# A 16-expert block: the loop over pairs of experts written out, and the last rows finished and waited for in another way

## Chip, core and metric

The kernel runs on one core of one Trainium2 chip. A core has five engines with an instruction stream each: TensorE (PE), VectorE (DVE), ScalarE (ACT), GpSimd (POOL) and SyncE (SP). The metric is the time in microseconds from the start of the program to its end on that core; the median of several runs counts.

## What is computed

One encoder layer over two sequences of 512 and 1024 tokens, width 1024: a mixer of attention and a state-space scan, a layer norm, then a feed-forward part in which each of 16 experts chooses its tokens, and a second layer norm. Only the feed-forward part and what follows it are touched:

```
aff = softmax((h @ w_router), axis=-1)
gate_vals, tok_idx = lax.top_k(aff.T, cap)              # per expert: 64 and 128 tokens of the two sequences
xg = h[tok_idx]
hid = silu(einsum('ecd,edf->ecf', xg, w_gate)) * einsum('ecd,edf->ecf', xg, w_up)
out = einsum('ecf,efd->ecd', hid, w_down) * gate_vals[..., None]
y = zeros_like(h).at[tok_idx.reshape(-1)].add(out.reshape(-1, d))
x = layer_norm(ALPHA * x + y, ln2_g, ln2_b)
```

`d` is 1024 and each expert's inner width is 2816, that is 22 chunks (`FCH`) of 128.

## The kernel before

`stage_experts` (from L1806) does the feed-forward part. Operands are float32 split into a high part and a remainder (`whi`, `wlo`; `xgT`, `hid` hold both), so that one product is made of several matmuls.

**An expert.** On TensorE it has 22 gate-and-up chunks (`gate_up`, L2043 and L2044, into `gu`) and 22 down chunks (`down`, L2055 to L2059, into `dns` and `dnp`). After chunks 0 and 1 it transposes the next expert's gathered tokens (`fill_tokens`, L2031 and L2032); these write into the banks of `dns`, so they wait (`row_done`) until the expert before has had its results read out. That read-out is `rows`: four ScalarE multiplications (L2172, L2175) and two VectorE operations (L2277) which stand at the start of the next expert, ahead of its first chunk. ScalarE copies each weight tile to `whi` (L2142), VectorE makes `wlo` (L2248), and SyncE loads 1056 weight tiles of 512 KB in a loop of its own. GpSimd gathers tokens and scatters results with indirect transfers.

**Loops.** The helper `experts` is used by TensorE, ScalarE and VectorE. Expert 0 and expert 15 are written out; experts 1 to 14 are a hardware loop (`Fori`, L1906) of seven turns with two experts in its body, so each of the three engines jumps back six times, at the ends of experts 2, 4, 6, 8, 10 and 12. Inside each expert the chunks 4 to 21 are a second hardware loop (L1915), three turns of six chunks.

**The end.** While expert 15 runs, GpSimd loads the accumulated rows tile by tile and ScalarE and VectorE normalise all 12 tiles as if expert 15 had chosen nothing. The rows that expert 15 did choose (`base_s`, 128 rows, and `base_p`, 64 rows) are done again at the very end by `last_rows`: VectorE adds expert 15's results (L2300; L2301 and L2304), ScalarE makes the mean (L2180) and the sum of squares (L2184), GpSimd the root in two steps (L1990, L1992), VectorE applies `gain` (L2282) and `shift` (L2287), and GpSimd writes the rows over the stored ones with two indirect transfers (L2022), after the stores of the 12 tiles have landed. GpSimd then waits for these two (`fix_out`). The stage closes (L1806) with a drain of each engine and a barrier over all five.

Of the kernel before, what the change touches and what calls it, by code (L numbers as in the profile page):

```python
# [1784 lines left out]
def stage_experts(nc, dram, res):  # L1785
# [20 lines left out]
    with ExitStack() as ctx:  # L1806
# [31 lines left out]
        rstd = m.sb("rstd", [P, NT + 2])  # L1838

# [60 lines left out]
        fix_out = m.sem("fix_out")  # L1900
        block = ctx.enter_context(nc.Block())
# [35 lines left out]
        def _(pool):  # L1937
# [48 lines left out]
            def root(n, ps=P):  # L1986
                of = (slice(0, ps), slice(n, n + 1))
# [4 lines left out]
                pool.tensor_tensor(rstd[of], rstd[of], half[0:ps], ALU.pow).then_inc(rstd_ready, 1)  # L1992
# [30 lines left out]
            pool.wait_ge(fix_out, 32)  # L2023
# [113 lines left out]
        def _(act):  # L2137
# [39 lines left out]
            def mean(n, of, ps=P):  # L2177
                if n >= 2:
                    act.wait_ge(var_ready, n - 1)
                act.activation(junk[n % 2][0:ps], of, ACT.Identity, scale=-1.0 / D, accum_out=nmean[0:ps, n:n + 1]).then_inc(mean_ready, 1)  # L2180

            def variance(n, of, ps=P):
                act.wait_ge(mean_ready, n + 1)
                act.activation(junk[n % 2][0:ps], of, ACT.Square, bias=nmean[0:ps, n:n + 1], accum_out=var[0:ps, n:n + 1]).then_inc(var_ready, 1)  # L2184
# [9 lines left out]
            def last_rows():  # L2194
# [17 lines left out]
        def _(dve):  # L2212
# [67 lines left out]
            def gain(n, of, ps=P):  # L2280
                dve.wait_ge(var_ready, n + 1)
                dve.scalar_tensor_tensor(of, of, nmean[0:ps, n:n + 1], ln[0:ps, 0, :], ALU.add, ALU.mult).then_inc(gained, 1)  # L2282

            def shift(n, of, ps=P):
                dve.wait_ge(gained, n + 1)
                dve.wait_ge(rstd_ready, n + 1)
                dve.scalar_tensor_tensor(of, of, rstd[0:ps, n:n + 1], ln[0:ps, 1, :], ALU.mult, ALU.add).then_inc(o_ready, 1)  # L2287
# [9 lines left out]
            def last_rows():  # L2297
                dve.wait_ge(gran_mm, GR * EXPERTS)
                dve.wait_ge(base_in, 32)
                dve.scalar_tensor_tensor(base[0][:], flat(dns), res["gates"][0][:, LAST:], base[0][:], ALU.mult, ALU.add).then_inc(y_ready, 1)  # L2300
# [3 lines left out]
                dve.tensor_tensor(base[1][:], base[1][:], plo[:], ALU.add).then_inc(y_ready, 1)  # L2304
                for i in range(2):
                    gain(NT + i, base[i][:], rows_of[i])
                    shift(NT + i, base[i][:], rows_of[i])
# [180 lines left out]
```

## Time and profile before

| | us |
|---|---|
| runs: 3512.11, 3512.74, 3518.86; median | 3512.74 |
| the profiled execution's own time | 3510.34 |
| its span, first to last instruction | 3508.2 |
| TensorE busy | 3376.6 (96%) |
| VectorE busy | 2343.7 (67%) |
| ScalarE busy | 1902.0 (54%) |
| GpSimd busy | 433.9 (12%) |
| mean granted TensorE clock | 0.983 of full speed |

The span is 2.1 us shorter than the time of the same execution, so a change of the span is read as the same change of the time. Expert 0's first matmul starts at 1019 us, expert 15's last at 3485.6 us: the feed-forward part is 70% of the span.

### The profile page before, as it was taken

To read this page: it belongs to the slowest core of one execution; us is meant where nothing else is said; L and a number is where in the kernel's file an instruction comes from. 1 tells how busy PE (TensorE), PEld (TensorE's weight loads), DVE (VectorE), ACT (ScalarE), POOL (GpSimd) and SP (SyncE) were. 2 spreads that over 40 slices of the span, in tenths; PEclk is the share of its full clock that TensorE was granted. 3 is DMA by queue.
4 is the path that set the end of the run, shared out by engine and by line. 5 is a ranking of instruction groups with operands and counts; after the bars stand their busy time and mean duration, and the time that the engine had idled before them with its cause. 6 is when DMAs were issued, how large, how long until landed. Compare 5 with 4: busy or idle time off the path is not lost.

```text
span 3508.2 us, 61800 instructions
## 1 busy us (share of the span) xinstructions
PE 3376.6 (96%) x20362; PEld 3094.5 (88%) x20362; DVE 2343.7 (67%) x3845; ACT 1902.0 (54%) x3335; POOL 433.9 (12%) x412
## 2 busy tenths in 40 slices
PE   8999989889959999999999999999999999999997
PEld 6889789678859999898989989898998989899996
DVE  6522167887777667676767767676776767676687
ACT  4222167433336556565655656565565656566576
POOL 0011066433210000000000001000000000000013
PEclk9999989999979999999999999999999999999998
DMA  4234254244356777677777777767777777776786
GB/s 169 83 110 162 78 120 122 59 149 152 123 178 234 238 234 237 226 240 243 235 232 237 235 234 233 241 234 235 235 238 235 223 239 234 238 235 227 237 287 226
DMA packets 247712, 712.92 MB, mean 203 GB/s; under 512 B 53600, under 2 KB 68896, under 8 KB 247232
## 3 DMA queue, kind: packets, MB, share of 16 engines
q1 hardware_dynamic: 230400, 650.54, 56.1%
q0 software_dynamic: 17088, 59.53, 5.9%
q8 instruction: 124, 2.03, 0.2%
q14 instruction: 100, 0.82, 0.1%
HBM read 648.00 MB, written 61.96 MB: 202 GB/s over the span
## 4 chain that ended last, share of the span: by engine, by line
PE 69%; issue 1%; DVE 1%; ACT 0%; DMA 0%; POOL 0%; DVEq 0%; ACTq 0%; POOLq 0%
PE moe_gu L2043 31%; PE moe_gu L2044 14%; PE moe_dns L2055 5%; PE moe_dns L2057 5%; PE moe_dnp L2058 5%; PE moe_dnp L2059 5%; PE moe_dns L2056 5%; PE moe_dns L2031 0%; PE moe_dns L2032 0%; DMA moe_xg_p<-tmp_h,moe_grow_p 0%; DVE rtr_found L2377 0%; DVE rtr_affT L2379 0%; DVE rtr_found L2375 0%; ACT moe_whi L2142 0%; DVE moe_og_p L2277 0%
## 5 line engine op out<-in xcount | busy, mean ns | idle before, releaser
L2043 PE MATMUL moe_gu<-moe_xgT,moe_whi 128*128 128x384 f32 x5632 | 1622.9, 362 | 7.5 <-issue 3.4
L2248 DVE TENSOR_TENSOR moe_wlo<-moe_raw,moe_whi 128x1024 fp32r<-128x1024 f32 x1056 | 1290.6, 1224 | 459.0 <-ACT moe_whi L2142 454.8
L2044 PE MATMUL moe_gu<-moe_xgT,moe_wlo 128*128 128x192 f32 x5632 | 1408.7, 250 | 0.0
L2142 ACT CAST moe_whi<-moe_raw 128x1024 fp32r<-128x1024 f32 x1056 | 1106.8, 1048 | 385.6 <-PE moe_dnp L2059 377.0
L2044 PEld LDWEIGHTS moe_gu<-moe_xgT,moe_wlo 128*128 128x128 f32 x5632 | 1076.8, 191 | 0.4
L2043 PEld LDWEIGHTS moe_gu<-moe_xgT,moe_whi 128*128 128x128 f32 x5632 | 1058.6, 188 | 10.8 <-issue 4.7
L1956 POOL DMA_INDIRECT tmp_acc<-moe_og_s,moe_srow_s x15 | 25.8, 1721 | 2090.5 <-ACT moe_og_s L2175 1388.1
L2055 PE MATMUL moe_dns<-moe_whi,moe_hid 128*128 128x512 f32 x704 | 275.9, 392 | 0.0
L2058 PE MATMUL moe_dnp<-moe_whi,moe_hid 128*128 128x512 f32 x704 | 275.6, 392 | 0.0
L2057 PE MATMUL moe_dns<-moe_wlo,moe_hid 128*128 128x512 f32 x704 | 275.6, 391 | 0.0
L2059 PE MATMUL moe_dnp<-moe_wlo,moe_hid 128*128 128x512 f32 x704 | 275.5, 391 | 0.0
L2056 PE MATMUL moe_dns<-moe_whi,moe_hid 128*128 128x512 f32 x704 | 275.4, 391 | 0.0
L2155 ACT CAST moe_hid<-moe_prod 128x192 f32 (+1 forms) x352 | 124.2, 353 | 147.1 <-DVE moe_prod L2257 146.1
L2149 ACT COPY rtr_found<-moe_gu 128x384 f32<-128x384 f32 x176 | 84.5, 480 | 211.0 <-PE moe_gu L2044 210.6
L2149 ACT COPY moe_part<-moe_gu 128x384 f32<-128x384 f32 x176 | 84.3, 479 | 201.8 <-PE moe_gu L2044 201.6
L2254 DVE TENSOR_TENSOR moe_guv<-moe_gu,moe_part 128x384 f32<-128x384 f32 x176 | 98.1, 557 | 123.1 <-ACT moe_part L2149 122.5
L2254 DVE TENSOR_TENSOR moe_guv<-moe_gu,rtr_found 128x384 f32<-128x384 f32 x176 | 98.1, 557 | 121.2 <-ACT rtr_found L2149 121.2
L238 PE MATMUL prj_ps<-prj_whi,prj_xhi 128*128 128x512 f32 (+1 forms) x480 | 170.0, 354 | 0.0
L239 PE MATMUL prj_ps<-prj_wlo,prj_xhi 128*128 128x512 f32 (+1 forms) x480 | 168.5, 351 | 0.0
L240 PE MATMUL prj_ps<-prj_whi,prj_xlo 128*128 128x512 f32 (+1 forms) x480 | 167.9, 350 | 0.0
L2059 PEld LDWEIGHTS moe_dnp<-moe_wlo,moe_hid 128*128 128x128 f32 x704 | 132.2, 188 | 29.1
L2057 PEld LDWEIGHTS moe_dns<-moe_wlo,moe_hid 128*128 128x128 f32 x704 | 132.2, 188 | 29.0
(318 smaller groups left out, 4397.0 us busy)
## 6 DMA issues: line engine op xcount, KB each, us to landing
moe_raw<-in_w_ffn SPq DMA_DIRECT2D x1056, 512.0 KB
res_early<-in_w_in SPq DMA_DIRECT2D x10, 1024.0 KB, 5.2
tmp_qkT<-prj_share POOLq DMA_DIRECT2D x24, 256.0 KB, 2.6
res_early<-tmp_qkT SPq DMA_DIRECT2D x16, 384.0 KB, 6.8
res_early<-tmp_xbc SPq DMA_DIRECT2D x12, 512.0 KB, 3.8
res_early<-in_x SPq DMA_DIRECT2D x12, 512.0 KB, 5.3
tmp_h<-res_early SPq DMA_DIRECT2D x12, 512.0 KB, 2.6
tmp_acc<-res_early SPq DMA_DIRECT2D x12, 512.0 KB, 4.0
```

The lines of the kernel that those rows point to most:

```text
L238: pe.matmul(out, hi, mhi, start=(k == 0), stop=False)
L2043: pe.matmul(out[:, a, 0:2 * CAP], whi[c][:, j, :], x, start=(j == 0), stop=False)
L2044: mm = pe.matmul(out[:, a, 0:CAP], wlo[c][:, j, :], x[:, 0:CAP], start=False, stop=(j == KD - 1))
L2055: pe.matmul(dns[:, n, :], hid[:, k, S_HI], hi[:, cols], start=first, stop=False)
L2056: pe.matmul(dns[:, n, :], hid[:, k, S_LO], hi[:, cols], start=False, stop=False)
L2057: pe.matmul(dns[:, n, :], hid[:, k, S_HI], lo[:, cols], start=False, stop=last)
L2058: pe.matmul(dnp[:, n, :], hid[:, k, P_BOTH], hi[:, cols], start=first, stop=False)
L2059: mm = pe.matmul(dnp[:, n, :], hid[:, k, P_BOTH], lo[:, cols], start=False, stop=last)
L2142: act.copy(whi[c][:], raw[c][:]).then_inc(hi_done, 1)
L2149: act.copy(part[s][:], gu[s][:, :, CAP:2 * CAP]).then_inc(part_out, 1)
L2248: dve.tensor_tensor(wlo[c][:], raw[c][:], whi[c][:].bitcast(F32), ALU.subtract).then_inc(lo_done, 1)
L2254: dve.tensor_tensor(guv[s][:], gu[s][:, :, 0:CAP], part[s][:], ALU.add).then_inc(summed, 1)
```

## The change

It has two parts. `experts` no longer makes a hardware loop: each of the three engines gets 16 experts one after the other. The loops over chunks inside an expert, SyncE's loop and GpSimd's loop stay. At the end, the two additions of `last_rows` also give the row sums (`accum_out`), from which VectorE makes two multiples of the negative mean with small operations; ScalarE's pass for the mean goes, the sum of squares is scaled so that VectorE only adds the epsilon, and GpSimd's root is one operation. The wait for the tiles' stores stands ahead of the roots now. The wait for the last two transfers moves from GpSimd to SyncE. Line numbers after L1838 move by one and more.

```diff
+        fix = m.sb("fix", [P, 6])
...
         def experts(eng, body):
 
-            body(0, 0, True, False)
-            with eng.Fori(0, EXPERTS // 2 - 1) as ee:
-                for q in range(2):
-                    body(2 * ee + 1 + q, 1 - q, False, False)
-            body(EXPERTS - 1, 1, False, True)
+            for e in range(EXPERTS):
+                body(e, e % 2, e == FIRST, e == LAST)
...
             sp.wait_ge(lo_done, BUFS + GR * EXPERTS)
+            sp.wait_ge(fix_out, 32)
...
-            for i in range(2):
-                root(NT + i, rows_of[i])
             for c in range(RBUF):
                 pool.wait_ge(o_out[c], 16 * NT // RBUF)
+            def last_root(i):
+                of = (slice(0, rows_of[i]), slice(NT + i, NT + i + 1))
+                pool.wait_ge(fix_eps, i + 1)
+                pool.tensor_tensor(rstd[of], var[of], half[0:rows_of[i]], ALU.pow).then_inc(fix_rstd, 1)
+
+            for i in range(2):
+                last_root(i)
...
-            pool.wait_ge(fix_out, 32)
...
+                act.wait_ge(var_ready, NT)
                 for i in range(2):
-                    act.wait_ge(y_ready, i + 1)
-                    mean(NT + i, base[i][:], rows_of[i])
-                    variance(NT + i, base[i][:], rows_of[i])
+                    ps = rows_of[i]
+                    act.wait_ge(fix_mean, 2 * i + 2)
+                    act.activation(junk[i][0:ps], base[i][:], ACT.Square, bias=fix[0:ps, 3 * i + 2:3 * i + 3], scale=D ** -0.5,
+                                   accum_out=var[0:ps, NT + i:NT + i + 1]).then_inc(fix_var, 1)
...
+                def means(i):
+                    ps = rows_of[i]
+                    dve.wait_ge(y_ready, i + 1)
+                    for c, by in ((1, -1.0 / D), (2, -1.0 / D * D ** -0.5)):
+                        dve.tensor_scalar(fix[0:ps, 3 * i + c:3 * i + c + 1], fix[0:ps, 3 * i:3 * i + 1], by, None, ALU.mult).then_inc(fix_mean, 1)
+
+                def normed(i):
+                    ps, n = rows_of[i], NT + i
+                    dve.wait_ge(fix_mean, 2 * i + 2)
+                    dve.wait_ge(fix_var, i + 1)
+                    dve.tensor_scalar(var[0:ps, n:n + 1], var[0:ps, n:n + 1], LN_EPS / ALPHA ** 2, None, ALU.add).then_inc(fix_eps, 1)
+                    dve.scalar_tensor_tensor(base[i][:], base[i][:], fix[0:ps, 3 * i + 1:3 * i + 2], ln[0:ps, 0, :], ALU.add, ALU.mult).then_inc(gained, 1)
+                    dve.wait_ge(fix_rstd, i + 1)
+                    dve.wait_ge(gained, n + 1)
+                    dve.scalar_tensor_tensor(base[i][:], base[i][:], rstd[0:ps, n:n + 1], ln[0:ps, 1, :], ALU.mult, ALU.add).then_inc(o_ready, 1)
...
-                dve.tensor_tensor(base[1][:], base[1][:], plo[:], ALU.add).then_inc(y_ready, 1)
+                dve.scalar_tensor_tensor(base[1][:], base[1][:], 1.0, plo[:], ALU.mult, ALU.add,
+                                         accum_out=fix[0:NP_, 3:4]).then_inc(y_ready, 1)
```

**ScalarE where expert 2 ends.** Before, these rows are the end of the loop's body; behind the branch stands, in the program's order, expert 15, and a jump goes back to expert 1's copy of the same read-out.

```order
L2142 CAST moe_whi<-moe_raw 128x1024
L1906 REGISTER_ALU
L1906 COMPARE_AND_BRANCH
L2172 ACTIVATE moe_plo<-moe_dnp,moe_gate 64x512 x2
L2175 ACTIVATE moe_og_s<-moe_dns,rtr_gates_s 128x512 x2
```

After, the same place between two experts:

```order
L1917 COMPARE_AND_BRANCH
L2149 CAST moe_whi<-moe_raw 128x1024 x22
L2179 ACTIVATE moe_plo<-moe_dnp,moe_gate 64x512 x2
L2182 ACTIVATE moe_og_s<-moe_dns,rtr_gates_s 128x512 x2
L2156 COPY moe_part<-moe_gu 128x384
```

The branch of the outer loop is gone, and so are the register steps of the expert's number; the branch left (L1917) is that of the chunk loop. TensorE and VectorE read the same way.

**VectorE at the end of the program.** Before:

```order
L2300 SCALAR_TENSOR_TENSOR moe_base_s<-moe_dns,rtr_gates_s,moe_base_s 128x1024
L2301 SCALAR_TENSOR_TENSOR moe_base_p<-moe_dnp,rtr_gates_p,moe_base_p 64x1024
L2304 TENSOR_TENSOR moe_base_p<-moe_base_p,moe_plo 64x1024
L2282 SCALAR_TENSOR_TENSOR moe_base_s<-moe_base_s,moe_nmean,moe_ln 128x1024
L2287 SCALAR_TENSOR_TENSOR moe_base_s<-moe_base_s,moe_rstd,moe_ln 128x1024
L2282 SCALAR_TENSOR_TENSOR moe_base_p<-moe_base_p,moe_nmean,moe_ln 64x1024
L2287 SCALAR_TENSOR_TENSOR moe_base_p<-moe_base_p,moe_rstd,moe_ln 64x1024
```

After:

```order
L2325 SCALAR_TENSOR_TENSOR moe_base_s,moe_fix<-moe_dns,rtr_gates_s,moe_base_s 128x1024
L2311 TENSOR_SCALAR moe_fix<-moe_fix 128x1 x2
L2328 SCALAR_TENSOR_TENSOR moe_base_p<-moe_dnp,rtr_gates_p,moe_base_p 64x1024
L2331 SCALAR_TENSOR_TENSOR moe_base_p,moe_fix<-moe_base_p,moe_plo 64x1024
L2311 TENSOR_SCALAR moe_fix<-moe_fix 64x1 x2
L2317 TENSOR_SCALAR moe_var<-moe_var 128x1
L2318 SCALAR_TENSOR_TENSOR moe_base_s<-moe_base_s,moe_fix,moe_ln 128x1024
L2321 SCALAR_TENSOR_TENSOR moe_base_s<-moe_base_s,moe_rstd,moe_ln 128x1024
L2317 TENSOR_SCALAR moe_var<-moe_var 64x1
L2318 SCALAR_TENSOR_TENSOR moe_base_p<-moe_base_p,moe_fix,moe_ln 64x1024
L2321 SCALAR_TENSOR_TENSOR moe_base_p<-moe_base_p,moe_rstd,moe_ln 64x1024
```

The seven large operations keep their order; six small ones are put between them, and two of the large ones also write a row sum into `moe_fix`.

**GpSimd at the end.** Before, four small operations, then the two transfers, behind which GpSimd waits until they have landed:

```order
L1990 TENSOR_SCALAR moe_rstd<-moe_var 128x1
L1992 TENSOR_TENSOR moe_rstd<-moe_rstd,moe_half 128x1
L1990 TENSOR_SCALAR moe_rstd<-moe_var 64x1
L1992 TENSOR_TENSOR moe_rstd<-moe_rstd,moe_half 64x1
L2022 DMA out<-moe_base_s,moe_srow_s 1536x1024
L2022 DMA out<-moe_base_p,moe_srow_p 1536x1024
L1806 UNCONDITIONAL_BRANCH
```

After:

```order
L2023 TENSOR_TENSOR moe_rstd<-moe_var,moe_half 128x1
L2023 TENSOR_TENSOR moe_rstd<-moe_var,moe_half 64x1
L2030 DMA out<-moe_base_s,moe_srow_s 1536x1024
L2030 DMA out<-moe_base_p,moe_srow_p 1536x1024
L1806 UNCONDITIONAL_BRANCH
```

Two of the four small operations are gone, and nothing is waited for between the second transfer and the branch to the stage's end.

## Rows read from the trace of the kernel before

**Rows 1.** The page: its head and busy times by engine.

```profile
span 3508.2 us, 61800 instructions
PE 3376.6 (96%) x20362; PEld 3094.5 (88%) x20362; DVE 2343.7 (67%) x3845; ACT 1902.0 (54%) x3335; POOL 433.9 (12%) x412
```

**Rows 2.** Waits of PE from 1100 to 3480 us: total us, times, longest.

```profile
PE moe_dns L2031 <- DVE moe_og_p L2277: 4.0, 4, 1.5
PE moe_gu L2043 <- issue: 3.4, 3, 1.2
PE moe_dns L2031 <- ACT moe_og_s L2175: 3.3, 2, 2.4
PE moe_gu L2043 <- DVE moe_wlo L2248: 2.9, 3, 1.0
```

**Rows 3.** Windows: expert 1 alone; first matmuls of expert 1 to expert 15.

```profile
1175.01:1327.98 152.97, 152.97 (x942) 143.91 (x940) 107.69 (x161) 92.74 (x140) 7.51 (x8) 1.00 0.74 236
1175.01:3334.58 2159.57, 2145.92 (x13161) 2015.90 (x13160) 1507.45 (x2241) 1298.26 (x1960) 101.23 (x108) 1.00 0.73 235
```

**Rows 4.** Timeline of PE, starts of experts 3 and 2.

```profile
1482.22 0.44 PE L2043 MATMUL moe_gu<-moe_xgT,moe_whi 128*128 128x384 f32 x1 [1.12 <-issue]
...
1488.37 0.30 PE L2031 MATMUL moe_dns<-moe_identr,moe_xg_s 128*128 128x128 f32 x1 [1.33 <-DVE moe_og_p L2277]
...
1332.54 0.27 PE L2031 MATMUL moe_dns<-moe_identr,moe_xg_s 128*128 128x128 f32 x1
```

**Rows 5.** Start of expert 3: the chain, and ScalarE's timeline.

```profile
1482.36 4.22 issue
...
1484.09 1.26 ACT L2172 ACTIVATE moe_plo<-moe_dnp,moe_gate 64x512 f32<-64x512 f32 x2 [1.90 <-issue]
```

**Rows 6.** DMA queues that carry instructions, 1480 to 1495 us, a jump back.

```profile
q14 instruction: 4, 0.03, 0.7%
q8 instruction: 1, 0.02, 0.4%
```

**Rows 7.** The same queues, 1046.3 to 1073.6 us: first turn of expert 0's chunk loop.

```profile
q8 instruction: 1, 0.02, 0.3%
q14 instruction: 2, 0.02, 0.1%
```

**Rows 8.** Timelines of VectorE and GpSimd at the end.

```profile
3486.05 1.28 DVE L2300 SCALAR_TENSOR_TENSOR moe_base_s<-moe_dns,rtr_gates_s,moe_base_s 128x1024 f32<-128x1024 f32 x1 [3.88 <-PE moe_dnp L2059]
...
3488.55 1.22 DVE L2304 TENSOR_TENSOR moe_base_p<-moe_base_p,moe_plo 64x1024 f32<-64x1024 f32 x1
...
3489.82 1.28 DVE L2282 SCALAR_TENSOR_TENSOR moe_base_s<-moe_base_s,moe_nmean,moe_ln 128x1024 f32<-128x1024 f32 x1
...
3491.24 0.56 POOL L1992 TENSOR_TENSOR moe_rstd<-moe_rstd,moe_half 128x1 f32<-128x1 f32 x1
3491.90 1.28 DVE L2287 SCALAR_TENSOR_TENSOR moe_base_s<-moe_base_s,moe_rstd,moe_ln 128x1024 f32<-128x1024 f32 x1 [0.80 <-POOL moe_rstd L1992]
...
3493.10 1.27 DVE L2282 SCALAR_TENSOR_TENSOR moe_base_p<-moe_base_p,moe_nmean,moe_ln 64x1024 f32<-64x1024 f32 x1
3493.32 1.47 POOL L1992 TENSOR_TENSOR moe_rstd<-moe_rstd,moe_half 64x1 f32<-64x1 f32 x1
3494.89 1.34 DVE L2287 SCALAR_TENSOR_TENSOR moe_base_p<-moe_base_p,moe_rstd,moe_ln 64x1024 f32<-64x1024 f32 x1 [0.52 <-POOL moe_rstd L1992]
...
3497.06 0.95 POOL L2022 DMA_INDIRECT out<-moe_base_p,moe_srow_p  x1 [0.99 <-DVE moe_base_p L2287]
```

**Rows 9.** VectorE: an accumulator's read-out at 446 us, a small operation at 1004 us.

```profile
446.45 0.08 DVE L845 DVE_READ_ACCUMULATOR2_ANT res_tab<- 128x1 f32 x1
...
1004.53 0.15 DVE L2227 TENSOR_SCALAR rtr_gates_p<-moe_dnp 64x16 f32<-64x16 f32 x1
```

**Rows 10.** GpSimd's closing drains, last stage and first: ns min/median/max, first and last start.

```profile
L1806 POOLq DRAIN  x1: 7501/7501/7501, 3500.5 to 3500.5; - x1
...
L115 POOLq DRAIN  x1: 4132/4132/4132, 433.6 to 433.6; - x1
```

More of the change, by code:

```diff
@@ L1984, in load, with root @@
                 pool.dma_start(r[n % RBUF][:], dram["acc"][P * n:P * n + P, :]).then_inc(r_in[n % RBUF], 16)
-            def root(n, ps=P):
-                of = (slice(0, ps), slice(n, n + 1))
+            def root(n):
+                of = (slice(0, P), slice(n, n + 1))
                 pool.wait_ge(var_ready, n + 1)
@@ L1991, in root @@
                 pool.wait_ge(rstd_tmp, n + 1)
-                pool.tensor_tensor(rstd[of], rstd[of], half[0:ps], ALU.pow).then_inc(rstd_ready, 1)
+                pool.tensor_tensor(rstd[of], rstd[of], half[:], ALU.pow).then_inc(rstd_ready, 1)
             def store(n):
@@ L2175, in rows, with mean, variance @@
                     act.mul(og[0][:, cols], dns[:, n, :], res["gates"][0][:, bass.ds(e, 1)]).then_inc(row_done, 1)
-            def mean(n, of, ps=P):
+            def mean(n, of):
                 if n >= 2:
                     act.wait_ge(var_ready, n - 1)
-                act.activation(junk[n % 2][0:ps], of, ACT.Identity, scale=-1.0 / D, accum_out=nmean[0:ps, n:n + 1]).then_inc(mean_ready, 1)
-            def variance(n, of, ps=P):
+                act.activation(junk[n % 2][:], of, ACT.Identity, scale=-1.0 / D, accum_out=nmean[:, n:n + 1]).then_inc(mean_ready, 1)
+            def variance(n, of):
                 act.wait_ge(mean_ready, n + 1)
-                act.activation(junk[n % 2][0:ps], of, ACT.Square, bias=nmean[0:ps, n:n + 1], accum_out=var[0:ps, n:n + 1]).then_inc(var_ready, 1)
+                act.activation(junk[n % 2][:], of, ACT.Square, bias=nmean[:, n:n + 1], accum_out=var[:, n:n + 1]).then_inc(var_ready, 1)
             def between(at):
@@ L2278, in rows, with gain, shift @@
                                              ALU.mult, ALU.add).then_inc(row_done, 1)
-            def gain(n, of, ps=P):
+            def gain(n, of):
                 dve.wait_ge(var_ready, n + 1)
-                dve.scalar_tensor_tensor(of, of, nmean[0:ps, n:n + 1], ln[0:ps, 0, :], ALU.add, ALU.mult).then_inc(gained, 1)
-            def shift(n, of, ps=P):
+                dve.scalar_tensor_tensor(of, of, nmean[:, n:n + 1], ln[:, 0, :], ALU.add, ALU.mult).then_inc(gained, 1)
+            def shift(n, of):
                 dve.wait_ge(gained, n + 1)
                 dve.wait_ge(rstd_ready, n + 1)
-                dve.scalar_tensor_tensor(of, of, rstd[0:ps, n:n + 1], ln[0:ps, 1, :], ALU.mult, ALU.add).then_inc(o_ready, 1)
+                dve.scalar_tensor_tensor(of, of, rstd[:, n:n + 1], ln[:, 1, :], ALU.mult, ALU.add).then_inc(o_ready, 1)
             def between(at):
@@ L2297, in last_rows @@
             def last_rows():
+                def means(i):
[12 more added lines that the diff above has]
+                    dve.scalar_tensor_tensor(base[i][:], base[i][:], rstd[0:ps, n:n + 1], ln[0:ps, 1, :], ALU.mult, ALU.add).then_inc(o_ready, 1)
                 dve.wait_ge(gran_mm, GR * EXPERTS)
                 dve.wait_ge(base_in, 32)
-                dve.scalar_tensor_tensor(base[0][:], flat(dns), res["gates"][0][:, LAST:], base[0][:], ALU.mult, ALU.add).then_inc(y_ready, 1)
+                dve.scalar_tensor_tensor(base[0][:], flat(dns), res["gates"][0][:, LAST:], base[0][:], ALU.mult, ALU.add,
+                                         accum_out=fix[:, 0:1]).then_inc(y_ready, 1)
+                means(0)
                 dve.scalar_tensor_tensor(base[1][:], flat(dnp)[0:NP_], res["gates"][1][:, LAST:], base[1][:], ALU.mult, ALU.add).then_inc(y_head, 1)
@@ L2303, in last_rows @@
                 dve.wait_ge(plo_ready, WIDE * LAST + 1)
-                dve.tensor_tensor(base[1][:], base[1][:], plo[:], ALU.add).then_inc(y_ready, 1)
+                dve.scalar_tensor_tensor(base[1][:], base[1][:], 1.0, plo[:], ALU.mult, ALU.add,
+                                         accum_out=fix[0:NP_, 3:4]).then_inc(y_ready, 1)
+                means(1)
                 for i in range(2):
-                    gain(NT + i, base[i][:], rows_of[i])
-                    shift(NT + i, base[i][:], rows_of[i])
+                    normed(i)
             def first_split(n):
```

4 lines of the change are left out of this document (added).

## Prediction, made before the changed kernel was run

> **What bounds the kernel now.** I read the head of the page first [rows 1]: TensorE is busy for 96% of the span, so time is won only where it stands still, or behind its last matmul. The waits of TensorE over experts 1 to 15 show all its idle time there [rows 2]: twelve waits, six ahead of L2043 (3.4 + 2.9 us) and six ahead of L2031 (4.0 + 3.3 us), 13.6 us. The reader is to see the counts: six and six, as many as the outer loop jumps back, though fourteen experts begin in that stretch. Next, windows: expert 1, which has the jump neither ahead of it nor behind it, takes 152.97 us and TensorE is busy for all of it; from expert 1's first matmul to expert 15's, fourteen experts, it is 2159.57 us [rows 3]. Fourteen times 152.97 is 2141.6, so 18.0 us are lost. This is more than the 13.6 of idle time, which starts only at a matmul's modelled end; the total is measured from start to start and holds whatever follows a wait as well, so I take 18.0.
>
> The timeline shows the two places [rows 4]. Expert 3's first matmul starts after 1.12 us idle, and its L2031 after 1.33 us more; in expert 2, reached without a jump, L2031 follows with no idle time. What is late is read in the chain at that place [rows 5]: behind VectorE's branch there are 4.22 us in which it waits for nothing that the profile shows, and ScalarE stands 1.90 us in the same way before it can read out the previous expert. The transposes wait for that read-out. In those 15 us the queues that carry instructions move four blocks for the smaller engines and one for TensorE [rows 6]: each engine fetches the head of the loop's body after it has jumped, and stands until it is there.
>
> **Part 1, the loop written out.** It removes six jumps on each of three engines and adds no operation to any of them. Each border between experts becomes what the one between experts 1 and 2 is: the next instructions lie behind the last ones. The worth is the 18.0 us above, if three things hold.
>
> First, code in a row is fetched in time. Expert 1 runs through its 152.97 us without a wait of TensorE, and it is such code. So is the entry to expert 15, behind which rows 2 have no wait either. Nothing else hides it: TensorE has no slack.
>
> Second, the chunk loops must not begin to fetch at their jumps. Their code now stands at fifteen places instead of three or four. In the first turn of expert 0's chunk loop the queues bring three blocks [rows 7], that is, each of the three engines crosses into a new block inside the loop; the second and third turns, the 55 us behind, bring none, and expert 1's loop costs nothing. A loop that lies across a border of blocks is thus kept whole. The Trainium skill, page Runtime: NRT & Kernel Launch, section on instruction fetch mechanics, says that a taken branch whose target is outside a window of two pages forces a fetch before execution goes on. The long jump agrees with it; the chunk loops show no such fetch. Its price, if new places of the loops did fall out of the window, is the rival on the slower side below.
>
> Third, what ends earlier must not meet anything. GpSimd's gathers and scatters and SyncE's loads follow the three engines by semaphores, and in expert 1 they keep up at the full pace. A shift of 18 us moves all of it together. Cost of this part elsewhere: 0. Its bounds: the whole 18.0, or, if ScalarE's and VectorE's delay had a cause other than the jump, only the first kind of gap, 6.3 of 13.6 us idle, 8.3 us.
>
> **Part 2, the last rows.** Times from the start of L2300, all from [rows 8]. Before: L2300 at 0, L2304 at 2.50, gain of base_s 3.77, shift 5.85, gain of base_p 7.05, shift 8.84, end 10.18, last transfer issued from 11.01 to 11.96. Two pitches are needed: a large VectorE operation that waits for nothing starts 1.20 us after the one before (3491.90 to 3493.10), one that waits for it 1.27 (3488.55 to 3489.82).
>
> After: the row sum needs an accumulator's read-out, 0.08 us, hidden in the pitch in the only row of its kind; the small operations take 0.15 us but follow each other at about 0.08 [rows 9]. The nearest rows are other shapes, so each is an estimate. L2325 at 0; its two small ones at 1.31 and 1.39; L2328 at 1.47; L2331 1.30 later, 2.77; its small ones at 4.08 and 4.16; the epsilon 4.24; gain of base_s 4.32. That is 0.55 later than before: 0.27 for the small ones ahead of L2328, the rest for the others. ScalarE's square for base_s needs only the first mean and is over by then.
>
> The root: GpSimd gets it about 0.2 us into the gain. While VectorE runs a large operation, GpSimd's small one is held: 1.47 us, ending 0.42 us behind VectorE's gain, against 0.56 us where VectorE was idle [rows 8]. So it ends at 4.32 + 1.28 + 0.42 = 6.02, and the shift starts at 6.12 (before 5.85). Then the epsilon of base_p at 7.32, gain 7.40, end 8.68, root 9.10, shift 9.20 (before 8.84). The chain becomes 0.36 us longer: what is saved on ScalarE's pass is not on the path, since VectorE's own seven operations are, and six small ones join them. Bounds: if the root isn't held, each shift follows its gain at 1.28 + 0.03, and the chain is some 1.0 us shorter than my sum; if an operation with a row sum were slower, longer.
>
> For that the Trainium skill has a rule, page Vector Engine (DVE) Microarchitecture Reference, section on points that are easy to get wrong: a scalar_tensor_tensor with two non-bf16 SBUF sources halves throughput, as no port is left for the accumulator. L2331 is such an operation. The trace has none with a row sum; without one, L2282 reads two float32 tiles from SBUF in 1.28 us, just as L2300 does with one in PSUM [rows 8]. By the row nothing is added; by the rule about 1.3 us.
>
> **Part 2, who waits for the stores.** Before, GpSimd's last issue ends at 3498.01; it waits until the rows have landed, and its drain starts at 3500.5 and takes 7.5 us [rows 10]. All other engines wait for that drain at the barrier. Queued behind GpSimd's wait is only this drain. Now the wait is SyncE's, whose queue is otherwise empty by then, and the drain starts at once: 2.5 - 0.1 = 2.4 us earlier. If it takes 7.5 us again, it ends 7.5 us later and well behind the landing, so SyncE's wait costs 0. What such a drain does is not in the trace. The nearest row is the first stage's: begun at 433.6, with its last transfer just issued, it took 4.1 us, with 70 GpSimd transfers in that stage by the program and 91 in the last, 66 of them indirect. A drain that first waited for the landing and then took as long as the last one would be longer than that. I take the full 2.4 and keep 0 as the other end.
>
> **The sum.** Against the profiled execution, 3510.34: -18.0 + 0.4 - 2.4 = -20.0, so 3490.3. The runs' median is 2.4 us above that execution, the lowest 1.8. Part of that scatter may lie in the gaps that go, so I add half: **3491.5 us**, 0.6% under 3512.74. A measurement of this kernel tells about 0.2%, 7 us, from no change.
>
> **The rivals.**
> - *Only the first kind of gap goes.* ScalarE and VectorE must still start the read-out late. For it speaks that their delay differs (1.90 and 4.22 us), against it that both stand behind the jump for nothing visible. 3510.3 - 8.3 - 2.0 + 1.2 = 3501.2. Chance 0.10.
> - *The drain waits for the transfers itself*, and the 2.4 us stay: 3493.9. For it: its 7.5 us are unexplained. Chance 0.10, and the rest of the sum as above.
> - *Slower: chunk loops that fetch at their jumps.* There are fifteen experts with two jumps back each, 30 on each engine. At the price of an outer jump, 18.0 / 6 = 3.0 us, all of them cost 90 us: about 3581; from seven such jumps on the 20 us are gone. Against it stand rows 7 and the fact that the first turn crossed a border on every engine. Chance 0.04. By the rule of the Trainium skill named above, a loop within two pages is kept and only one that reaches out of them would pay this.
> - *The loop's writing out does not do what it says*: blocks come as late in straight code as behind a jump, once or twice per expert. Expert 1 speaks against it. Then about 3508. Chance 0.04.
>
> **How the numbers follow.** The forecast, with both variants of the root and of the row sum in it, has 0.72; its own range is 3488 to 3496 (3490.3 less 1.0 and less some scatter; 3492.7 with all of the 2.4 and 1.3 more, and scatter). The other cases leave 0.28, of which the drain's 3493.9 lies inside. To hold eight in ten I go up to the first rival: **3487 to 3502**. Faster by over 0.2% (under 3505.7): forecast, both first rivals: 0.92. Same: 0.04. Slower: 0.04.
>
> **What the changed kernel's profile would show.** TensorE's waits in the experts, but for expert 0's, are gone; from expert 1's first matmul to expert 15's it is 2142 us; no VectorE or ScalarE operation at an expert's start has idle time put down to issue; instruction blocks come singly. From the first end operation to the shift's end 10.5 us; GpSimd's drain starts within 0.2 us of its last issue and lasts 7.5 us. The prediction is wrong if a wait shows at other places in the experts, if jumps of L1917 have instruction blocks beside them in their second or third turn, or if the drain grows by what it starts earlier.

## The result and the profile after

| | before | after |
|---|---|---|
| median of 6 runs each | 3512.19 us | 3494.68 us |
| lowest to highest | 3508.07 to 3518.86 | 3490.89 to 3497.92 |
| profiled execution, its span | 3510.34, 3508.2 | 3490.89, 3489.1 |

The ratio is 0.995, with a 95% interval of 0.9939 to 0.996: 17.5 us less, 14 to 21. The forecast of 3491.5 is 3.2 us under the median, inside the range.

The page after, its head and the rows of the instruction queues (queue, kind: packets, MB, share), against [rows 1]:

```profile
span 3489.1 us, 60146 instructions
PE 3369.8 (97%) x20362; PEld 3091.4 (89%) x20362; DVE 2344.5 (67%) x3853; ACT 1898.4 (54%) x3331; POOL 432.2 (12%) x410
...
q8 instruction: 112, 1.84, 0.2%
q14 instruction: 65, 0.52, 0.0%
```

The same two rows of the page before:

```profile
q8 instruction: 124, 2.03, 0.2%
q14 instruction: 100, 0.82, 0.1%
```

TensorE executes the same 20362 matmuls. The instruction queues bring fewer blocks although the code is longer: 112 and 65, where it was 124 and 100. That fits a loop body that is brought in anew at every turn: writing it out adds no blocks to fetch.

Windows of the kernel after, expert 1 alone and the first matmuls of expert 1 to expert 15 (columns: length, busy us of PE, PEld, DVE, ACT, POOL, granted clock, DMA share, GB/s), against [rows 3]:

```profile
1175.97:1328.94 152.97, 152.97 (x942) 143.92 (x941) 107.79 (x161) 92.66 (x140) 7.30 (x8) 1.00 0.75 236
1175.97:3317.50 2141.53, 2141.53 (x13162) 2014.81 (x13160) 1508.15 (x2241) 1297.23 (x1960) 102.68 (x108) 1.00 0.75 237
```

2141.53 is fourteen times 152.97 to within 0.05 us, and TensorE is busy for all of it. Against [rows 2], where twelve waits stood, the list of TensorE's waits over that stretch is empty. The only idle time of L2050 on the whole page is 1.2 us, and that is expert 0's.

Timelines of VectorE and GpSimd at the end, after, against [rows 8] (brackets: idle time before, and what ended it):

```profile
3468.97 1.28 DVE L2325 SCALAR_TENSOR_TENSOR moe_base_s<-moe_dns,rtr_gates_s,moe_base_s 128x1024 f32<-128x1024 f32 x1 [3.89 <-PE moe_dnp L2066]
3470.17 0.08 DVE L2325 DVE_READ_ACCUMULATOR moe_base_s<-moe_dns,rtr_gates_s,moe_base_s 128x1 f32 x1
...
3471.72 1.22 DVE L2331 SCALAR_TENSOR_TENSOR moe_base_p<-moe_base_p,moe_plo 64x1024 f32<-64x1024 f32 x1
...
3473.12 0.14 DVE L2317 TENSOR_SCALAR moe_var<-moe_var 128x1 f32<-128x1 f32 x1
3473.18 1.27 DVE L2318 SCALAR_TENSOR_TENSOR moe_base_s<-moe_base_s,moe_fix,moe_ln 128x1024 f32<-128x1024 f32 x1
...
3473.43 1.44 POOL L2023 TENSOR_TENSOR moe_rstd<-moe_var,moe_half 128x1 f32<-128x1 f32 x1 [7.52 <-DVE moe_var L2317]
...
3477.88 1.28 DVE L2321 SCALAR_TENSOR_TENSOR moe_base_p<-moe_base_p,moe_rstd,moe_ln 64x1024 f32<-64x1024 f32 x1 [0.44 <-POOL moe_rstd L2023]
...
3478.04 2.07 POOL L2030 DMA_INDIRECT out<-moe_base_s,moe_srow_s  x1 [0.19 <-issue]
3480.41 0.95 POOL L2030 DMA_INDIRECT out<-moe_base_p,moe_srow_p  x1 [0.30 <-issue]
```

And the closing drains with SyncE's waits near the end (for a wait: total, times, longest), against [rows 10]:

```profile
L1806 POOLq DRAIN  x1: 9100/9100/9100, 3479.8 to 3479.8; - x1
...
SPq L1937 <- DMA out<-moe_base_p,moe_srow_p: 38.8, 1, 38.8
```

Read the drain against the issue above it: the drain's record begins at 3479.8, while the first transfer's issue is still going on (3478.04 + 2.07 = 3480.11), and ahead of the second one. It ends at 3488.9. Its length in the record is therefore no measure; what counts is its end behind the end of the last issue, 3480.41 + 0.95 = 3481.36: 7.5 us. Before, it began behind the landing and also took 7.5 us. The last stretch, from the first large addition's start to the span's end, is 3489.05 - 3468.97 = 20.1 us, where it was 3508.2 - 3486.05 = 22.15 [rows 8, 1].

The whole balance of the two profiled executions: experts 1 to 14, -18.04; last stretch, -2.07; start of expert 0, 1019.14 before and 1020.28 after, +1.14 in code that is the same; expert 0 with its transients, -0.18; sum -19.15, spans -19.1.

### The profile page after: what moved, and what is told of

It is laid out like the page before. It is cut to its first block, busy times and chain, and to the rows that moved or that the text cites. A ratio compares the mean times of both kernels' runs of the same rounds, so it can differ in the third digit from the quotient of the medians.

```text
span 3489.1 us, 60146 instructions
## 1 busy us (share of the span) xinstructions
PE 3369.8 (97%) x20362; PEld 3091.4 (89%) x20362; DVE 2344.5 (67%) x3853; ACT 1898.4 (54%) x3331; POOL 432.2 (12%) x410
## 4 chain that ended last, share of the span: by engine, by line
PE 70%; DVE 1%; DMA 0%; POOL 0%; issue 0%; POOLq 0%; ACT 0%; DVEq 0%
PE moe_gu L2050 32%; PE moe_gu L2051 14%; PE moe_dns L2062 5%; PE moe_dns L2064 5%; PE moe_dnp L2065 5%; PE moe_dnp L2066 5%; PE moe_dns L2063 5%; PE moe_dns L2038 0%; PE moe_dns L2039 0%; DMA moe_xg_p<-tmp_h,moe_grow_p 0%; DVE rtr_found L2405 0%; DVE rtr_affT L2407 0%; DVE rtr_found L2403 0%; POOL moe_rstd L2023 0%; POOL moe_xg_s L1950 0%
## 5 line engine op out<-in xcount | busy, mean ns | idle before, releaser
L2050 PE MATMUL moe_gu<-moe_xgT,moe_whi 128*128 128x384 f32 x5632 | 1619.2, 361 | 1.2 <-DVE moe_xgT L2279 1.2
L2050 PEld LDWEIGHTS moe_gu<-moe_xgT,moe_whi 128*128 128x128 f32 x5632 | 1057.3, 188 | 2.1 <-DVE moe_xgT L2279 1.4
```

Source lines behind the costliest of these rows:

```text
L2050: pe.matmul(out[:, a, 0:2 * CAP], whi[c][:, j, :], x, start=(j == 0), stop=False)
```

## Experiments

"Last stretch" is always from the start of the first large addition at the end to the span's end, and "fourteen experts" from expert 1's first matmul to expert 15's. Both are free of the scatter of the first thousand microseconds, so the profiles are compared by them; several kernels below were run only once, and for these the profile is all that counts. In kernels without jumps the fourteen experts repeat to the hundredth (2141.53 us in three profiles); with the six jumps on all engines they took 2159.57 and 2156.75 us in two, so a difference of some 3 us between kernels that jump isn't clear of the scatter.

**The two parts alone.** Each kernel is the one before with one part of the change.

```diff
-            body(0, 0, True, False)
-            with eng.Fori(0, EXPERTS // 2 - 1) as ee:
-                for q in range(2):
-                    body(2 * ee + 1 + q, 1 - q, False, False)
-            body(EXPERTS - 1, 1, False, True)
+            for e in range(EXPERTS):
+                body(e, e % 2, e == FIRST, e == LAST)
```

The first kernel has this and nothing else of the change, the second has all else and not this.

> The kernel before with only the experts' loop written out; the end is the old one. Theory A (each jump back of the outer loop costs 3.0 us, nothing else changes): TensorE has no wait in experts 1 to 15, from expert 1's first matmul to expert 15's it is 2141.6 us instead of 2159.6, and the runs are 18.0 us under the kernel before, ratio 0.9949. Theory B (part of the gain in the profile is chance, and the end carries a share of the measured 17.5 us): 13 to 15 us, ratio 0.996 to 0.9963. The last stretch, from the start of L2300's operation to the span's end, stays at 22.1 us by both.

> The new end alone, with the loop over pairs of experts as in the kernel before. Theory A: the last stretch is 20.1 us instead of 22.1, the runs are 2.1 us under the kernel before, ratio 0.9994, too little to be told from none with certainty. Theory B (the arithmetic of the end brings something and the wait nothing, or the other way about, with the same sum): the same time; the profile tells them apart, by when the last shift ends (10.2 us after the stretch's start in both kernels so far) and by when the drain of GpSimd starts. The experts still show twelve waits, 18 us.

Loop alone: 3497.16 us against 3513.41, ratio 0.9954 (0.9937 to 0.9971). End alone: 3509.96, ratio 0.9989 (0.9978 to 1.0), 3.5 us by the medians with an interval that touches no change. Windows of the fourteen experts, loop alone and then end alone:

```profile
1180.35:3321.88 2141.53, 2141.53 (x13161) 2014.81 (x13160) 1508.94 (x2241) 1297.42 (x1960) 101.95 (x108) 1.00 0.75 237
```

```profile
1180.60:3337.35 2156.75, 2144.25 (x13162) 2014.23 (x13161) 1507.43 (x2241) 1297.92 (x1960) 101.19 (x108) 1.00 0.75 235
```

The loop gives all of the gain in the experts, to the hundredth; the last stretch is 22.15 us with the loop alone and 20.1 with the end alone. In the profiles the parts add up. The end-only kernel also shows that the price of a jump is not fixed: six of them cost 15.2 us here and 18.0 before. Most of the difference lies in one expert of the kernel before, the eleventh. Windows of experts 3 and 11, before:

```profile
1482.22:1636.81 154.59, 153.26 (x940) 144.00 (x941) 107.35 (x160) 91.79 (x139) 8.42 (x8) 1.00 0.74 234
2716.13:2873.39 157.26, 154.88 (x941) 145.62 (x941) 107.50 (x160) 91.64 (x140) 6.98 (x8) 0.99 0.72 229
```

In expert 11 TensorE is busy 1.6 us longer with the same work: behind its wait of 2.38 us ahead of the transposes the granted clock fell. No expert of the end-only kernel shows that. So the 18.0 us hold 1.6 us of a lower clock that a wait brought with it.

**Which engine's jump costs what.** The helper tests which engine it writes for; the diff is that of TensorE alone, and the two others have `eng is not nc.tensor` and `eng is nc.vector` in its place.

```diff
         def experts(eng, body):
-            for e in range(EXPERTS):
-                body(e, e % 2, e == FIRST, e == LAST)
+            if eng is nc.tensor:
+                for e in range(EXPERTS):
+                    body(e, e % 2, e == FIRST, e == LAST)
+            else:
+                body(0, 0, True, False)
+                with eng.Fori(0, EXPERTS // 2 - 1) as ee:
+                    for q in range(2):
+                        body(2 * ee + 1 + q, 1 - q, False, False)
+                body(EXPERTS - 1, 1, False, True)
```

The end of the program is that of before in all three.

> The kernel before, with the loop over experts written out on TensorE alone; ScalarE and VectorE still jump back six times. Theory A (the wait ahead of the first matmul is TensorE's own fetch, the one ahead of the transposes that of the two others): six waits ahead of L2043 are gone, six ahead of L2031 stay, and they grow, since the time by which TensorE was late itself no longer covers the others: between a saving of 7 us with waits as before and no saving at all. Theory B (all engines wait for one cause, say the queue that brings instructions): both kinds shrink together, a saving of 9 us or more.

> The kernel before, with the loop over experts written out on ScalarE and VectorE and kept on TensorE. Theory A: the six waits ahead of L2031 are gone and the six ahead of L2043 stay at 1.3 us from matmul to matmul beyond the usual: 2159.6 - 10.7 = about 2149 us from expert 1's first matmul to expert 15's. Theory B (one common cause): both kinds shrink, below 2149. If TensorE's own fetch cost nothing, 2141.6.

> The kernel before, with the loop over experts written out on VectorE alone. In the wait ahead of the transposes both ScalarE (2.4 us behind its jump, four operations of the read-out) and VectorE (3.3 to 4.5 us behind its own) can be last. Theory A (VectorE's fetch, the longest, sets it): that wait is nearly gone, and from expert 1's first matmul to expert 15's it is about 2149 to 2151 us, as with both written out. Theory B (ScalarE's fetch sets it as well, since its operations stand ahead of VectorE's): most of it stays, 2154 us or more.

TensorE written out alone, its waits from 1100 to 3480 us and windows of the fourteen experts, of expert 5, of expert 7, and of 5 us behind expert 5's wait:

```profile
PE moe_dns L2035 <- DVE moe_og_p L2281: 10.4, 5, 2.7
PE moe_dns L2035 <- ACT moe_og_s L2179: 1.8, 1, 1.8
```

```profile
1189.54:3349.20 2159.66, 2147.49 (x13162) 2020.37 (x13160) 1507.30 (x2241) 1297.61 (x1960) 100.58 (x108) 1.00 0.75 235
...
1803.51:1960.21 156.70, 154.71 (x941) 145.52 (x940) 107.70 (x161) 92.62 (x140) 7.04 (x8) 0.99 0.74 232
2113.18:2268.49 155.31, 153.16 (x942) 143.97 (x941) 107.59 (x161) 92.71 (x140) 8.43 (x8) 1.00 0.75 234
1811.50:1816.50 5.00, 5.00 (x27) 5.00 (x26) 3.59 (x7) 1.97 (x4) 3.36 (x2) 0.69 0.73 115
```

The rows of the instruction queues, TensorE written out and then ScalarE and VectorE:

```profile
q8 instruction: 112, 1.84, 0.2%
q14 instruction: 100, 0.82, 0.1%
```

```profile
q8 instruction: 124, 2.03, 0.2%
q14 instruction: 64, 0.52, 0.1%
```

The waits of TensorE with ScalarE and VectorE written out (TensorE jumps), then with VectorE alone:

```profile
PE moe_gu L2047 <- DVE moe_wlo L2252: 3.4, 4, 1.0
PE moe_gu L2047 <- issue: 2.5, 2, 1.3
```

```profile
PE moe_gu L2047 <- issue: 4.7, 4, 1.3
PE moe_dns L2035 <- ACT moe_og_s L2179: 3.1, 4, 0.9
PE moe_gu L2047 <- DVE moe_wlo L2252: 1.8, 2, 1.1
```

| written out | waits ahead of gate-up | waits ahead of transposes | fourteen experts | of this, lower clock | blocks, q8 and q14 |
|---|---|---|---|---|---|
| none (before) | 6, 6.3 us | 6, 7.3 us | 2159.57 | 1.6 | 124, 100 |
| TensorE | 0 | 6, 12.2 us | 2159.66 | 4.7 | 112, 100 |
| VectorE | 6, 6.5 us | 4, 3.1 us | 2153.54 | 0 | 124, 82 |
| ScalarE, VectorE | 6, 5.9 us | 0 | 2149.03 | 0 | 124, 64 |
| all three | 0 | 0 | 2141.53 | 0 | 112, 65 |

"Lower clock" is the busy time of TensorE in the experts where the clock fell, less that of their like in the same kernel. The blocks show the fetches themselves: q8 brings fewer when TensorE stops jumping and only then, two for each of the six jumps; q14 brings three fewer per jump for VectorE and three for ScalarE.

Each kind of wait belongs to an engine, as the prediction read it: ahead of gate-up it is TensorE's own jump, ahead of the transposes the late read-out by VectorE and ScalarE. The two are in series, though. TensorE without its jump comes to the transposes about a microsecond sooner and waits there for the same read-out, so most of its 6.3 us turns up again: all its waits together are 12.2 us where they were 13.6. In three of these experts (5, 9, 13) the granted clock also fell behind the longer wait, for a while from the upper of its two levels, 2.4 GHz, to the lower, 1.2: its mean is 0.69 over 5 us in expert 5. TensorE was busy there for 154.71 us with work that took 153.16 in expert 7, at a mean of 1.00: 1.5 us, and 4.7 in the three experts together. That this kernel gained nothing at all is therefore a reading of one profile with three such falls, where the profile before has one; less the clock it would be some 3 us ahead. Length alone does not decide: the six waits were 1.7 to 2.7 us, and the one in expert 7 (2.15) was longer than that in expert 5 (1.99).

VectorE alone gives 6.0 us, between the two ends expected; ScalarE's fetch is a second cause for the same wait, which it sets in four of six cases once VectorE is on time. With ScalarE too it is 10.5 us, and TensorE on top of these 7.5 us. TensorE's share is thus 0 when it goes first (3 less the clock) and 7.5 when it goes last, so the sizes depend on the order. The time of the first kernel's only run, 3524.78, is no effect of the loop: its expert 0 starts at 1033.3 us, 14 us later than before, in code that is the same. Nothing is concluded from it. The other two ran once each, in 3504.82 us (ScalarE, VectorE) and 3509.02 (VectorE).

**Fewer jumps.** The kernel before with a body of four experts and three turns, so two jumps, at the ends of experts 4 and 8.

```diff
-            with eng.Fori(0, EXPERTS // 2 - 1) as ee:
-                for q in range(2):
-                    body(2 * ee + 1 + q, 1 - q, False, False)
-            body(EXPERTS - 1, 1, False, True)
+            with eng.Fori(0, 3) as ee:
+                for q in range(4):
+                    body(4 * ee + 1 + q, (1 + q) % 2, False, False)
+            for e in range(13, EXPERTS):
+                body(e, e % 2, False, e == LAST)
```

> The kernel before, with four experts in the loop's body and three turns, experts 13 and 14 written out: two jumps back on each engine instead of six. Theory A (a fixed price of 3.0 us for a jump of all three engines, nothing else): 2141.6 + 6.0 = 2147.6 us from expert 1's first matmul to expert 15's, with waits at the starts of experts 5 and 9 alone. Theory B (the price grows with the length of the body that is jumped over): more than 5 us for each jump.

```profile
PE moe_dns L2032 <- DVE moe_og_p L2278: 1.7, 2, 1.2
PE moe_gu L2044 <- issue: 1.2, 1, 1.2
PE moe_gu L2044 <- DVE moe_wlo L2249: 1.1, 1, 1.1
```

Two waits of each kind, at experts 5 and 9, nowhere else; fourteen experts take 2146.44, that is 4.9 us over 2141.53, or 2.5 us for each jump, though each now goes back over four experts instead of two; 3500.41 in its one run. The loss goes by the number of jumps, and not by the length of the body, as theory B had it.

**Who waits for the last transfers.** The changed kernel with the wait back on GpSimd.

```diff
-            sp.wait_ge(fix_out, 32)
...
+            pool.wait_ge(fix_out, 32)
```

> The changed kernel with the wait for the last two transfers moved back from SyncE to GpSimd, ahead of its closing drain. Theory A (the drain takes 7.5 us from the moment GpSimd is free, whether or not transfers are under way): the span ends 7.5 us after the wait's end, 2.4 to 2.6 us later behind the last issue than in the changed kernel, and the last stretch, from the start of L2325's operation to the span's end, is 22.6 us instead of 20.1. Theory B (the drain counts from the landing, and the 20.1 us came from elsewhere): 20.1 us again.

```profile
L1806 POOLq DRAIN  x1: 7501/7501/7501, 3488.4 to 3488.4; - x1
```

3498.12 in its one run. The last issue ends at 3485.72, the transfer lands at 3488.25, the drain takes 7.5 us behind it, and the last stretch is 22.8 us in place of 20.1: 2.7 us, which is the time from the last issue's end to the drain's start, 2.5 of it up to the landing. So this drain takes 7.5 us whether or not the last transfers are in flight, and the rival that it would wait for them by itself is refuted.

**What the drain's length goes by.** A drain of GpSimd more, at one or two places of the last stage (and, in the first of these kernels, one in the first stage, ahead of its last two stores).

```diff
             for n in range(2, RBUF):
                 load(n)
+            pool.drain()                       # e8, e10, e11
             root(0)
...
+            pool.drain()                       # e11, e12
             for c in range(RBUF):
                 pool.wait_ge(o_out[c], 16 * NT // RBUF)
```

> The changed kernel with two more drains of GpSimd: in the last stage ahead of the first root, where GpSimd is idle for some 9 us, and in the first stage ahead of the last two stores of v. Nothing is left out. Theory A (a closing drain works through the transfers that GpSimd issued since the last drain, 0.05 to 0.1 us each): the last closing drain has 20 of 91 left and shrinks from 7.5 us to below 2.5, so that SyncE's wait for the landing ends last and the last stretch is about 16 us instead of 20.1; the first stage's, with 2 of 70 left, shrinks from 4.1 us to about the landing, 2 us. Theory B (7.5 us is the price of a drain in that stage): 20.1 us again, and the drain in the middle costs 7.5 us too, hidden or not.

> The changed kernel once more, beside the three variants that follow, on the same chip and between the same runs of the kernel before. Expected: 0.993 to 0.997 of the kernel before (it was 0.995), and in its profile experts 1 to 14 in 2141.53 us, no wait of TensorE in them, and 20.1 us from the first of the last additions to the end of the span, with a closing drain on GpSimd that ends 7.5 us behind the end of the last transfer issue.

> The changed kernel with one drain of GpSimd more, set behind the loads with which the last stage's normalisation begins (the first of the two places of the run with both drains). Theory A, the closing drain goes by the transfers that GpSimd issued since its last drain: 24 stand in place of 90, the closing drain ends some 3.4 us behind the end of the last issue in place of 7.5, the last stretch is 16.0 us in place of 20.1, and the ratio to the changed kernel is 4.1 / 3495 = 0.12% lower, 0.9985 to 0.999. The drain that was set in the attention stage as well in the earlier run is left out here, and by A does nothing. Theory B, that other drain had a part in the gain: more than 16.5 us in the last stretch.

> As the variant before, and one more drain behind GpSimd's last ordinary store, in the 6 us in which it waits for the last additions. Theory A: 2 transfers stand before the closing drain; in the attention stage a closing drain with 3 took 2.1 us, so it ends before the last transfer has landed and SyncE has seen it, and the end is set by that landing: the last stretch is 15.2 to 15.6 us in place of 16.0. Theory B, the length of the closing drain goes by something else than the transfers since the last drain: 16.0 us again. The other risk is the added drain itself: if it is longer than the 6.6 us that GpSimd is idle there, the first power of the last rows starts late and the last stretch is longer than 16.0 us.

> The changed kernel with one drain more, behind the last ordinary store alone, so that this drain has 88 transfers behind it and the closing one 2. The drain with 66 transfers that stood behind the loads took 25.4 us while VectorE was at work on the experts; the closing drain of the changed kernel with 90 took 7.5 us past the last issue, with VectorE idle. Theory A, a drain's length goes by the transfers and by what else runs: this one takes at least 7.5 us, more than the 6.6 us in which GpSimd is idle there, delays the first power of the last rows by 1 to 18 us, and the last stretch is 16.5 to 34 us. Theory B, a drain here is as short as the closing one with few transfers: 15.2 to 16.0 us.

Three things in these expectations are miscounted. By the program and by the trace GpSimd issues 91 transfers in the last stage; 71 lie ahead of the drain before the norms (64 of them indirect) and 20 behind it, and between the two places of the added drains there are 18. For 90, 66, 24 and 88 read 91, 71, 20 and 89, as the first of the kernels was reckoned. And the drain added early in that kernel stands in the first stage, not in the attention stage, with two transfers behind it and not three.

GpSimd's closing drain with a drain ahead of the norms, and that drain itself (L2011); with both drains, the same two and the later one (L2019); with the later one alone (L2018):

```profile
L1806 POOLq DRAIN  x1: 4979/4979/4979, 3481.7 to 3481.7; - x1
...
L2011 POOLq DRAIN  x1: 26146/26146/26146, 3338.2 to 3338.2; - x1
```

```profile
L1806 POOLq DRAIN  x1: 4222/4222/4222, 3483.6 to 3483.6; - x1
...
L2019 POOLq DRAIN  x1: 3692/3692/3692, 3469.2 to 3469.2; - x1
```

```profile
L1806 POOLq DRAIN  x1: 4228/4228/4228, 3482.2 to 3482.2; - x1
...
L2018 POOLq DRAIN  x1: 7898/7898/7898, 3467.8 to 3467.8; - x1
```

The first stage's closing drain, in the changed kernel and in the first of these, and the closing drain of a stage in which GpSimd computes and issues no transfer, before:

```profile
L115 POOLq DRAIN  x1: 4127/4127/4127, 435.0 to 435.0; - x1
...
L115 POOLq DRAIN  x1: 2119/2119/2119, 435.0 to 435.0; - x1
...
L1276 POOLq DRAIN  x1: 662/662/662, 971.8 to 971.8; - x1
```

| | transfers since last drain | drain ends after last issue's end | last stretch | median (5 runs) | to before |
|---|---|---|---|---|---|
| changed, again | 91 | 7.5 us | 20.1 us | 3495.10 | 0.9953 |
| drain ahead of norms | 20 | 3.4 | 16.0 | 3490.81 | 0.994 |
| both | 2 | 2.6 | 15.3 | 3488.89 | 0.9933 |
| after the stores alone | 2 | 2.6 | 15.3 | 3489.28 | 0.9933 |

The first kernel, with the drain in the first stage too, had 16.0 us as well and 3486.28 in its one run; its closing drain ended 3.4 us behind the last issue, not below 2.5 as expected. Its drain in the first stage did nothing for the end, but it shows the same there: with two transfers since the last drain instead of 70 that stage's closing drain took 2.1 us instead of 4.1, as theory A of its expectation said. And it is the transfers that count, not the other work of GpSimd: in the stage without any (L1276) the drain ends at 972.5 us, 0.1 us behind GpSimd's last operation. The interval of the last two is 0.9919 to 0.9947, that of the changed kernel in the same set 0.9939 to 0.9967; they overlap, so it is the last stretch that shows the gain, not the medians; by the medians the best kernel is 6.2 us under the changed one and 24.4 under before, and the last stretch accounts for 4.8 of the 6.2. The later drains show the same dependence: with 18 transfers since the one before 3.1 us from the last issue's end, with 89 it was 7.3. What I had expected of the last kernel, at least one microsecond lost, did not come: its drain's record is 7.9 us long, but it ends 7.3 us behind the last store's issue, and GpSimd is free for 7.5 us there, from the end of the last store's issue to the first root, not 6.6. The root started 0.2 us later than without the drain (4.65 for 4.46 us into the last stretch) and ended at the same point, 5.90.

With two transfers the closing drain ends at 3487.83 and SyncE, which has waited for the landing, is ready 0.1 us later (its own drain starts at 3487.94). The drain's end and the landing are level now, so a further drain could win little; and with two transfers left it can't be told whether the drain itself waits for their landing. What the drain does with the transfers is not visible in a trace. That its length falls with their number since the last drain is shown. The number isn't all: the drain ahead of the norms has 71 behind it and ends only 22.6 us after the last issue (3338.2 + 26.1 against 3341.7). That they are mostly indirect can't be the reason, since the same 64 indirect ones are among the 89 that took 7.3. What differs is that the experts still run, with VectorE, ScalarE and the weights' loads; which of these makes it so long wasn't tried. It is covered by the experts, since GpSimd's first root waits longer than that for its data.

## Why the prediction was right

**The loop.** -18.0 predicted, -18.04 measured, and again 2141.53 us with the loop alone and in the changed kernel's second set. That it agrees to the hundredth is no proof of such accuracy: the 18.0 were read from the very profile with which the changed one is compared, and the end-only kernel, with the same jumps, lost 15.2. What the runs bear out is that all of the loss goes, whatever it is in an execution. The step that carried it was to take the price from the difference of two start-to-start times and not from the idle times, 13.6 us, and to see that waits came six and six. It also took in the 1.6 us of expert 11's lower clock, which the prediction did not see but counted with "whatever follows a wait". Its claims that straight code is fetched in time and that chunk loops go on without a fetch held: TensorE waits nowhere in 14 experts, with 28 jumps back inside them. Its bound on the lower side, that only the first kind of gap might go, was the wrong lower end in size: the gaps ahead of gate-up are worth nothing when they go alone, or some 3 us less the clock, since the wait ahead of the transposes takes them up, and 8.3 us was what I gave them.

**The transfers.** -2.4 predicted for the earlier drain. The drain did take 7.5 us again from where GpSimd is free. That point moved from 14.47 us after the start of the last stretch to 12.39: -2.1. The 0.3 between them comes from the first transfer's issue, 2.07 us in place of 1.09, so that the second could start only at 11.4 instead of 11.0; this was no step of the prediction. It is 2.07 in all eight profiles with the new end and 1.09 in all six with the old one, with the same data and operation; what makes it longer stays open.

**The arithmetic.** +0.36 predicted for the start of the last shift, +0.07 measured (8.91 for 8.84), and its end is at 10.19 for 10.18. So the new arithmetic brought nothing, and the 2.1 us of the end are the moved wait. The mis-sized terms are small ones: the small operations follow each other at 0.06 us and not 0.08, so that the gain of base_s starts at 4.21 and not 4.32; and from a gain to its shift it is 1.72 and 1.71 us, where I had 1.80. The root is held as assumed, and ends 0.42 us behind the gain; the shift follows it at 0.03, not 0.10. This sum was 0.3 us too high, which about made up for the issue. The rule of the Trainium skill weighed there, page Vector Engine (DVE) Microarchitecture Reference, section on points that are easy to get wrong, does not show here: L2331, with two float32 sources in SBUF and a row sum, took 1.22 us, as long as the addition without one that it replaced [rows 8].

**The scatter.** 1.2 us were added for the distance of the runs' median to the profiled execution. After, that distance is 3.8 us. It is not in the gaps that went: expert 0's first matmul starts between 1019.1 and 1033.3 us in the thirteen profiled executions that have the same code up to there, in which the mean granted clock is 0.92 to 0.93 from 400 to 1010 us, and everything behind it repeats to about three microseconds (the jumps). Against the profiled executions alone the prediction was 3490.3 for 3490.89, where the start of expert 0, 1.1 us later by scatter, makes most of the difference.

**The slower rival**, chunk loops that fetch at their jumps, is refuted. The instruction queues of the changed kernel during the whole of expert 3:

```profile
q8 instruction: 4, 0.07, 0.2%
q14 instruction: 2, 0.02, 0.1%
```

None of these blocks comes between 1520 and 1580 us, where the chunk loop of that expert jumps back on all three engines (by the distances in expert 0, between 1529 and 1537 us and again 27 us later), and 2141.53 leaves nothing to pay for.

## What to carry to other kernels

When a loop's jump costs something, count the waits against the jumps, take the price from start to start of equal units, and write out all engines that follow each other, since the waits are in series and one engine alone may give little or nothing. At a program's end, look at what every engine's drain stands behind: a wait for a transfer belongs on an engine whose drain is short (SyncE's took 7 ns here). And where GpSimd's drain is last, a drain of its own in an idle stretch before makes it shorter.

## What was not expected of the hardware

- A closing drain of GpSimd ends 7.5 us behind its last issue with 91 transfers since the last drain, 3.4 with 20 and 2.6 with 2; with 91 it takes 7.5 us too when it begins after the last has landed. A drain with 71 behind it, while the experts ran, ended 22.6 us behind its last issue.
- Its record can start before the issue ahead of it has ended (3479.8 against 3480.11 here), so its length is to be read from the last issue's end.
- A wait of TensorE of 1.99 us was followed by 5 us at a mean granted clock of 0.69 in one expert, which cost 1.5 us; behind one of 2.15 us in another the expert's mean stayed 1.00.
- A jump back over two experts costs 2.5 to 3.0 us in the three engines together (one over four experts 2.5), and brings 2 blocks for TensorE and 3 each for ScalarE and VectorE; jumps inside an expert, over six chunks, show no cost to TensorE.
